# High and low activation rows in one product of 512 columns, in the hidden projections of a two-part transformer

## The chip, the core and the metric

The kernel runs on one core of a Trainium2 chip. The metric is the device time of one execution in microseconds. Lower is better.

## The reference, cut to what matters

Two blocks of a transformer follow each other on 256 tokens of width 1024. The change touches three kinds of projection from width 1024 to a hidden width: gate and up of the SwiGLU (width 2816, two layers), and the first projection of an MLP with squared relu (width 4096, two layers of the second block, one of them also on a second stream of 256 context tokens).

```python
def swiglu(h, w_gate, w_up, w_down):
    return (jax.nn.silu(h @ w_gate) * (h @ w_up)) @ w_down
...
        h = rms_norm(x, ffn_norm[i]) * (1.0 + sc_f) + sh_f
        x = x + g_f * swiglu(h, ffn_w_gate[i], ffn_w_up[i], ffn_w_down[i])
```

The MLP of the second block is relu(h @ w1) squared, times w2. Attention of three kinds, a pooling mixer and the modulation vectors (a vector c times large matrices) make up the rest. All is float32.

## The kernel before, in words

**Products.** A float32 product is made of three in the faster type fp32r: each operand is split into a high part (rounded) and a low part (the rest), and high x high, high x low and low x high are summed in PSUM (`three`, L1582 to L1586). Activations are turned so that the model width lies on the partitions: `hT_hi` and `hT_lo`, each 128 x 8 (k) x 256 tokens.

**Weights.** They stream in units of 1 MB, in the order of the segments `segs`. SP fetches unit u into one of four slots `wraw` as soon as the unit four before has been split. ACT rounds it to `whi` (L556, two halves of 1024), DVE subtracts for `wlo` (L945, two halves). `whi` and `wlo` have two slots, so a split of unit u + 2 waits until TensorE is done with unit u (`unit_done`), and TensorE waits for `lo_ready` of each half.

**Hidden units.** A unit of a gate, up or first projection is 1024 x 256 weights: 8 k-tiles by 2 halves f of 128 hidden columns. `hidden_unit` (L1631) makes for each f and k one triple with 128 x 128 weights as the stationary and 256 tokens as the moving operand; the results of both f lie side by side in one bank, in turn banks 2, 0, 1, 3 (`H_BANKS`). In the first unit of a stage k is the outer loop, since `hT` comes in by k (`fed_wait`); there a matmul of zeros (L1644) starts the bank. Stages `up0` and `up1` have kind "pair": gate and up units alternate, 22 in each stage; ACT reads the gate's bank with silu into `hbuf` (L573), DVE multiplies the up's bank by it (L962). Stages `up20`, `up21` and `up3` have kind "up", 16 units each: ACT reads the bank with relu into `hbuf` (L578) and squares it into `hid` (L581).

**Order on ACT and DVE.** Both are strict sequences. In `stream` (ACT and DVE), step i is: split unit i + 2, then the output of unit i, then, where the stage carries vector units, the next ring transfer (ACT) or a bias sum (DVE). In the last two steps of a stage the output comes first, then the split of the first two down units. A down unit also needs `act_hi` (ACT, L552) and `act_lo` (DVE, L939), the split of 512 hidden values, ahead of its weights.

**Vector units.** A piece of the modulation vectors (8 matmuls on 1 MB from the `ring`, which ACT fetches) stands behind each of the first 12 units of `up0`, 20 of `up1`, 12 of `up21` and 4 of `down1`.

**Down.** `down_segment` starts its four banks (4, 5, 6, 2) with matmuls of zeros (L1676) once the hidden stage's last ACT step is done, then per unit 24 products with `act_hi` or `act_lo` as the stationary and 512 weight columns as the moving operand. Ahead of a hidden stage stands a norm: `norm` on PE (L1698) turns the rows through banks 6, 0, 1, 3 (`T_BANKS`).

Of the kernel before, what the change touches and what calls it, by code (L numbers as in the profile page):

```python
# [8 lines left out]
F32R = mybir.dt.float32r  # L9
BF16 = mybir.dt.bfloat16  # L10
I32 = mybir.dt.int32
ALU = mybir.AluOpType
# [79 lines left out]
def build(nc, x, c, positions, ada_w, ada_b, attn_norm, ffn_norm, ffn_w_gate, ffn_w_up, ffn_w_down,  # L92
# [6 lines left out]
    with stack:  # L99
# [13 lines left out]
        hT_hi = sb("hT_hi", [P, KT, S], F32R)  # L113
        hT_lo = sb("hT_lo", [P, KT, S], F32R)
# [56 lines left out]
        T_BANKS = (6, 0, 1, 3)  # L171
# [113 lines left out]
        hid_done, hact_done = sem("hid_done"), sem("hact_done")  # L285
# [72 lines left out]
        HT_STEPS = (0, 1, 2, 4, 6)  # L358
        PLAIN = (4, 6)
# [150 lines left out]
        def _(act):  # L510
# [52 lines left out]
            def hidden_out(s_, i):  # L563
# [3 lines left out]
                if s_["kind"] == "pair":  # L567
# [3 lines left out]
                    act.wait_ge(unit_done, u + 1)  # L571
                    act.wait_ge(hid_done, hid_base[tag] + n - 1)
                    nc.scalar.activation(hbuf[:, n % 2, :], ps[:, H_BANKS[i % 4], :], ACT.Silu).then_inc(hact_done, 1)  # L573
                else:
                    act.wait_ge(unit_done, u + 1)
# [75 lines left out]
            def norm_columns():  # L651
# [3 lines left out]
                for b in (1, 3):  # L655
# [3 lines left out]
                    for k in (2 * b, 2 * b + 1):  # L659
                        shift = 0.0 if n in PLAIN else modT[:, l, strm, f, 0, k:k + 1]  # L660
                        ins = nc.scalar.activation(full[:, k, :], ps[:, T_BANKS[b], (k % 2) * S:(k % 2 + 1) * S], ACT.Identity,
# [224 lines left out]
        def _(dve):  # L886
# [65 lines left out]
            def hidden_out(s_, i):  # L952

                if s_["kind"] != "pair" or i % 2 == 0:
                    return
                u = s_["base"] + i
                n = i // 2
                hb = hid_base[s_["name"][2:]]
# [96 lines left out]
            def norm_columns():  # L1055
# [10 lines left out]
                def modulated(k):  # L1066
                    src = ps[:, T_BANKS[k // 2], (k % 2) * S:(k % 2 + 1) * S]
# [456 lines left out]
        def _(pe):  # L1524
# [106 lines left out]
            def hidden_unit(s_, i):  # L1631

                u = s_["base"] + i
                hb = hid_base[s_["name"][2:]]
                unit_wait(u, 0)

                if s_["kind"] == "pair":
                    which, v = (hact_done if i % 2 == 0 else hid_done), hb + i // 2 - 1
                else:
                    which, v = hact_done, hb + i - 3  # L1640
                pe.wait_ge(which, v)
                zeroed = i == 0
                if zeroed:
# [391 lines left out]
```

## Time and profile before

| | |
|---|---|
| three runs | 1711.67, 1711.74, 1712.48 us, median 1711.74 |
| profiled execution | 1709.29 us, span in the profile 1707.2 us |
| granted TensorE clock, mean | 0.941 |
| busy: PE, PEld | 1549.2 us (91%), 1308.6 us (77%) |
| busy: DVE, ACT | 938.3 us (55%), 718.6 us (42%) |
| HBM read | 333.79 MB, 196 GB/s over the span |

The profile is one execution. PE is TensorE's matmuls, PEld its weight loads, DVE is VectorE, ACT is ScalarE, SP the engine that issues the weight transfers. A matmul's duration reaches from its start to the end of its pipeline, so durations overlap; their distances do not. An idle time stands in brackets with what ended it.

### The profile page before, as it was taken

The page shows a single profiled execution, that of the slowest core. Times are in us where ns is not written, and L with a number is a line of the kernel's source. Part 1 is how long each engine was busy: PE and PEld are TensorE (multiplying, and loading weights), DVE is VectorE, ACT ScalarE, POOL GpSimd, SP SyncE. Part 2 cuts the span into 40 slices and gives each one's busy share as a digit, 9 for nine tenths or more (in the row PEclk, how much of TensorE's full clock was granted, in tenths as well). Part 3 has the DMA queues.
Part 4 walks back from the last instruction along what each step waited for, and adds up shares of the span by engine and source line. Part 5 has one row for each costly group of instructions (what it writes and reads, how often), then busy time and mean ns, then how long its engine had stood idle before and what let it go on. Part 6 is the DMA issues. An engine that isn't in the chain of part 4 may idle for free.

```text
span 1707.2 us, 24515 instructions
## 1 busy us (share of the span) xinstructions
PE 1549.2 (91%) x10326; PEld 1308.6 (77%) x10326; DVE 938.3 (55%) x1609; ACT 718.6 (42%) x1098; POOL 0.2 (0%) x4
## 2 busy tenths in 40 slices
PE   3998789999898789999979999799998886999997
PEld 2766668898686559888759988688986764779986
DVE  3584545345669755334575455753456786363455
ACT  2353524334444424333435544344444543345543
POOL 0000000000000000000000000000000000000000
PEclk9997789999998889999979999899999898989999
DMA  9962157965544657997734655469655353545552
GB/s 370 368 240 99 50 173 266 306 201 178 185 149 157 213 173 251 306 306 254 241 111 151 195 174 190 142 210 305 205 195 172 124 172 123 173 124 177 171 195 86
DMA packets 165845, 336.42 MB, mean 197 GB/s; under 512 B 8160, under 2 KB 109160, under 8 KB 165480
## 3 DMA queue, kind: packets, MB, share of 16 engines
q1 hardware_dynamic: 138880, 230.90, 40.2%
q10 hardware_dynamic: 26856, 103.96, 18.0%
q8 instruction: 81, 1.33, 0.3%
q14 instruction: 28, 0.23, 0.0%
HBM read 333.79 MB, written 1.05 MB: 196 GB/s over the span
## 4 chain that ended last, share of the span: by engine, by line
PE 79%; DVE 14%; ACT 2%; issue 2%; DMA 2%; ACTq 0%; SPq 0%; DVEq 0%
PE ps L1584 22%; PE ps L1585 21%; PE ps L1586 21%; PE ps L1556 5%; DVE wlo L945 2%; PE ps L1715 2%; DVE res L1024 1%; DVE work L1022 1%; PE ps L1712 1%; PE ps L1812 1%; PE ps L1785 1%; ACT whi L556 1%; PE ps L1824 1%; DVE work L1109 1%; PE ps L1754 1%
## 5 line engine op out<-in xcount | busy, mean ns | idle before, releaser
L945 DVE TENSOR_TENSOR wlo<-wraw,whi 128x1024 fp32r<-128x1024 f32 (+1 forms) x424 | 498.1, 1216 | 415.1 <-ACT whi L556 414.6
L556 ACT ACTIVATE whi<-wraw 128x1024 fp32r<-128x1024 f32 (+1 forms) x424 | 423.7, 1047 | 472.5 <-PE ps L1586 452.6
L1584 PE MATMUL ps<-hT_hi,whi 128*128 128x256 f32 x1472 | 422.5, 287 | 0.0
L1585 PE MATMUL ps<-hT_lo,whi 128*128 128x256 f32 x1472 | 416.9, 283 | 0.0
L1586 PE MATMUL ps<-hT_hi,wlo 128*128 128x256 f32 x1472 | 416.5, 283 | 0.0
L1584 PEld LDWEIGHTS ps<-hT_hi,whi 128*128 128x128 f32 x1472 | 282.8, 192 | 20.2 <-issue 18.1
L1585 PEld LDWEIGHTS ps<-hT_lo,whi 128*128 128x128 f32 x1472 | 282.9, 192 | 0.0
L1586 PEld LDWEIGHTS ps<-hT_hi,wlo 128*128 128x128 f32 x1472 | 282.8, 192 | 0.0
L1584 PE MATMUL ps<-whi,act_hi 128*128 128x512 f32 x560 | 219.0, 391 | 0.0
L1585 PE MATMUL ps<-wlo,act_hi 128*128 128x512 f32 x560 | 218.1, 390 | 0.0
L1586 PE MATMUL ps<-whi,act_lo 128*128 128x512 f32 x560 | 217.9, 389 | 0.0
L1584 PE MATMUL ps<-whi,hT_hi 128*128 128x512 f32 (+2 forms) x416 | 163.3, 393 | 5.2 <-DVE hT_lo L1073 5.1
L1585 PE MATMUL ps<-wlo,hT_hi 128*128 128x512 f32 (+2 forms) x416 | 159.1, 382 | 0.0
L1586 PE MATMUL ps<-whi,hT_lo 128*128 128x512 f32 (+2 forms) x416 | 158.4, 381 | 0.0
L939 DVE TENSOR_TENSOR act_lo<-work,act_hi 128x512 fp32r<-128x512 f32 x70 | 48.5, 693 | 191.7 <-ACT whi L556 191.7
L1584 PEld LDWEIGHTS ps<-whi,act_hi 128*128 128x128 f32 x560 | 105.1, 188 | 25.6 <-issue 3.8
L552 ACT ACTIVATE act_hi<-work 128x512 fp32r<-128x512 f32 x70 | 44.2, 631 | 191.2 <-issue 170.0
L1586 PEld LDWEIGHTS ps<-whi,act_lo 128*128 128x128 f32 x560 | 105.1, 188 | 22.0
L1585 PEld LDWEIGHTS ps<-wlo,act_hi 128*128 128x128 f32 x560 | 105.1, 188 | 21.5
L1584 PEld LDWEIGHTS ps<-whi,hT_hi 128*128 128x128 f32 x416 | 79.7, 191 | 30.9 <-issue 8.7
L1556 PE MATMUL ps<-ring,cpad 128*32 128x256 f32 x1440 | 97.9, 390 | 2.0 <-DMA ring<-in_ada_w_dram 1.2
L1586 PEld LDWEIGHTS ps<-whi,hT_lo 128*128 128x128 f32 x416 | 79.2, 190 | 15.3
(200 smaller groups left out, 1319.6 us busy)
## 6 DMA issues: line engine op xcount, KB each, us to landing
wraw<-in_mlp_w_dram SPq DMA_DIRECT2D x96, 1024.0 KB, 5.4
ring<-in_ada_w_dram ACTq DMA_DIRECT2D x90, 1024.0 KB, 5.6
wraw<-in_ffn_w_gate_dram SPq DMA_DIRECT2D x22, 1024.0 KB, 6.2
wraw<-in_ffn_w_up_dram SPq DMA_DIRECT2D x22, 1024.0 KB, 6.2
wraw<-in_ffn_w_down_dram SPq DMA_DIRECT2D x22, 1024.0 KB, 4.9
wraw<-in_diff_w_in_dram SPq DMA_DIRECT2D x12, 1024.0 KB, 5.0
wraw<-in_attn_w_qkv_dram SPq DMA_DIRECT2D x12, 1024.0 KB, 5.1
wraw<-in_sp_w_in_dram SPq DMA_DIRECT2D x8, 1024.0 KB, 13.0
```

The source lines that it names most:

```text
L552: nc.scalar.activation(act_hi[:, u % 2, :], hid[:, at:at + 512], ACT.Copy)
L556: nc.scalar.activation(whi[:, u % 2, part], raw_view(u)[:, part], ACT.Copy).then_inc(hi_ready, 1)
L939: nc.vector.tensor_tensor(act_lo[:, u % 2, :], hid[:, at:at + 512], act_hi[:, u % 2, :].bitcast(F32), ALU.subtract)
L945: nc.vector.tensor_tensor(wlo[:, u % 2, part], raw_view(u)[:, part], whi[:, u % 2, part].bitcast(F32), ALU.subtract).then_inc(lo_ready, 1)
L1022: nc.vector.tensor_tensor(tmp[:, t, cols], ps[:, D_BANKS[q], :], gate_b[:, cols], ALU.mult).then_inc(dve_emptied, 1)
L1024: nc.vector.tensor_tensor(res[:, strm, t, cols], res[:, strm, t, cols], tmp[:, t, cols], ALU.add).then_inc(sem("res_ready"), 1)
L1109: return nc.vector.tensor_tensor(views[t], views[t], g.rearrange("p a (c d) -> p a c d", c=1).to_broadcast([P, a, b, width]), ALU.mult)
L1556: ins = mm(ps[32 * c_:32 * c_ + 32, ADA_BANK, 0:256], cpad[:, 0 if g < 12 else 1, kt, :], ring_view(r)[:, kk * D + 256 * c_:kk * D + 256 * ...
L1584: mm(dst, s_hi, m_hi, start=start, stop=False, skip_group_check=skip)
L1585: mm(dst, s_hi, m_lo, start=False, stop=False, skip_group_check=skip)
L1586: return mm(dst, s_lo, m_hi, start=False, stop=stop, skip_group_check=skip)
L1715: ins = nc.tensor.transpose(ps[:, T_BANKS[b], (k % 2) * S + t * P:(k % 2) * S + (t + 1) * P], xn[:, t, k * P:(k + 1) * P], ident)
```

## The change

`hT_hi` and `hT_lo` become two halves of one tile `hT`, so that one moving operand can cover both: for a k, 256 high and 256 low columns. In a hidden unit high weights times high and low activations is now one product of 512 columns, which fills a whole bank; low weights times high activations stays one of 256 columns, added to the bank's first half. The two halves of the bank have to be added. DVE does this as it reads: a reduce over pairs of values 256 columns apart, for both f (two banks), into `hbuf` (gate and first projections) or `hid` (up). ACT's silu and relu read `hbuf` instead of PSUM and wait for the new semaphore `hid_sum`; the product of gate and up is made from SBUF. A unit takes two banks, in turn (0, 1), (2, 3), (4, 5). So the third unit waits for the copies of the gate vector out of banks 4 and 5, a unit from the fourth on for the sum of the unit three before, the down stage for the second-last sum only, and the transposes ahead of a hidden stage use banks 6, 3, 2, 4 (the last of them with a wait for the gate copies). The first unit needs no matmul of zeros.

```diff
-        hT_hi = sb("hT_hi", [P, KT, S], F32R)
-        hT_lo = sb("hT_lo", [P, KT, S], F32R)
+        hT = sb("hT", [P, 2, KT, S], F32R)
+        hT_hi, hT_lo = hT[:, 0], hT[:, 1]
...
+        HIDDEN_BANKS = (0, 2, 4)
+        TO_ROWS, TO_HIDDEN = (6, 0, 1, 3), (6, 3, 2, 4)
...
+        def hidden_banks(i):
+
+            b = HIDDEN_BANKS[i % 3]
+            return ps[:, b:b + 2, :].rearrange("p f (a n) -> p f n a", a=2)
...
-                    act.wait_ge(unit_done, u + 1)
                     b = i % 2
-                    act.wait_ge(hid_done, hid_base[tag] + i - 1)
-                    nc.scalar.activation(hbuf[:, b, :], ps[:, H_BANKS[i % 4], :], ACT.Relu).then_inc(hact_done, 1)
+                    act.wait_ge(hid_sum, sum_base[tag] + i + 1)
+                    nc.scalar.activation(hbuf[:, b, :], hbuf[:, b, :], ACT.Relu).then_inc(hact_done, 1)
...
-                if s_["kind"] != "pair" or i % 2 == 0:
+                if s_["kind"] == "down":
                     return
...
                 dve.wait_ge(unit_done, u + 1)
-                dve.wait_ge(hact_done, hb + n + 1)
-                at = 512 * n
-                nc.vector.tensor_tensor(hid[:, at:at + 512], ps[:, H_BANKS[i % 4], :], hbuf[:, n % 2, :], ALU.mult).then_inc(hid_done, 1)
+                if pair and i % 2:
+                    dst = hid[:, 512 * n:512 * n + 512]
+                else:
+                    dve.wait_ge(hid_done, hb + n - 1)
+                    dst = hbuf[:, n % 2, :]
+                nc.vector.tensor_reduce(dst.rearrange("p (f n) -> p f n", f=2), hidden_banks(i), AX, ALU.add).then_inc(hid_sum, 1)
+                if pair and i % 2:
+                    dve.wait_ge(hact_done, hb + n + 1)
+                    dve.wait_ge(hid_sum, sb_ + i + 1)
+                    nc.vector.tensor_tensor(dst, dst, hbuf[:, n % 2, :], ALU.mult).then_inc(hid_done, 1)
...
-                pe.wait_ge(which, v)
-                zeroed = i == 0
-                if zeroed:
-                    mm(ps[:, H_BANKS[0], :], zero16[0:1, 0:P], zero16[0:1, :], start=True, stop=False, skip_group_check=True)
...
+                if i >= 3:
+                    pe.wait_ge(hid_sum, sum_base[s_["name"][2:]] + i - 2)
+                if i == 2:
+                    pe.wait_ge(*gate_out[0])
...
-                    ins = three(ps[:, H_BANKS[i % 4], f * S:(f + 1) * S], whi[:, u % 2, c0:c0 + P], wlo[:, u % 2, c0:c0 + P], hT_hi[:, k, :], hT_lo[:, k, :],
-                                k == 0 and not zeroed, k == KT - 1 and not zeroed, zeroed)
+                    bank = HIDDEN_BANKS[i % 3] + f
+                    mm(ps[:, bank, :], whi[:, u % 2, c0:c0 + P], hT[:, :, k, :], start=(k == 0), stop=False, skip_group_check=True)
+                    ins = mm(ps[:, bank, 0:S], wlo[:, u % 2, c0:c0 + P], hT_hi[:, k, :], start=False, stop=(k == KT - 1), skip_group_check=True)
...
-                pe.wait_ge(hact_done, hb)
+                pe.wait_ge(hid_sum, sum_base[tag] + by_name["up" + tag]["count"] - 1)
```

The order of instructions on ACT at the end of `up3`, from the split of unit 15 to that of the second down unit (`down3`), before:

```order
L556 ACTIVATE whi<-wraw 128x1024 [waits unit_done,raw_full3]
L556 ACTIVATE whi<-wraw 128x1024
L578 ACTIVATE hbuf<-ps 128x512 [waits hid_done,unit_done]
L581 ACTIVATE work<-hbuf 128x512 [waits hact_done]
L578 ACTIVATE hbuf<-ps 128x512 [waits hid_done,unit_done]
L581 ACTIVATE work<-hbuf 128x512 [waits hact_done]
L552 ACTIVATE act_hi<-work 128x512 [waits hid_done,unit_done,raw_full0]
```

And in the changed kernel:

```order
L569 ACTIVATE whi<-wraw 128x1024 [waits unit_done,raw_full3]
L569 ACTIVATE whi<-wraw 128x1024
L589 ACTIVATE hbuf<-hbuf 128x512 [waits hid_sum]
L592 ACTIVATE work<-hbuf 128x512 [waits hact_done]
L589 ACTIVATE hbuf<-hbuf 128x512 [waits hid_sum]
L592 ACTIVATE work<-hbuf 128x512 [waits hact_done]
L565 ACTIVATE act_hi<-work 128x512 [waits hid_done,unit_done,raw_full0]
```

The order is the same; relu reads `hbuf` and waits for DVE's sum instead of TensorE's unit.

DVE at the same place, in the changed kernel (`work` in `act_lo<-work` is the hidden row `hid`). Before, the rows L978 were not there:

```order
L956 TENSOR_TENSOR wlo<-wraw,whi 128x1024 [waits hi_ready] x2
L978 TENSOR_REDUCE hbuf<-ps 128x512 [waits hid_done,unit_done] x2
L950 TENSOR_TENSOR act_lo<-work,act_hi 128x512 [waits hi_ready]
L956 TENSOR_TENSOR wlo<-wraw,whi 128x1024
L956 TENSOR_TENSOR wlo<-wraw,whi 128x1024 [waits hi_ready]
L978 TENSOR_REDUCE hbuf<-ps 128x512 [waits hid_done,unit_done]
L950 TENSOR_TENSOR act_lo<-work,act_hi 128x512 [waits hi_ready]
```

The two reduces of units 13 and 14 stand between the split of unit 15 and that of the first down unit, the reduce of unit 15 between the splits of the first and the second down unit.

## Rows read from the trace of the kernel before

**Rows 1.** The page's chain that ended last, by engine and by line.

```profile
PE 79%; DVE 14%; ACT 2%; issue 2%; DMA 2%; ACTq 0%; SPq 0%; DVEq 0%
PE ps L1584 22%; PE ps L1585 21%; PE ps L1586 21%; PE ps L1556 5%; DVE wlo L945 2%; PE ps L1715 2%; DVE res L1024 1%; DVE work L1022 1%; PE ps L1712 1%; PE ps L1812 1%; PE ps L1785 1%; ACT whi L556 1%; PE ps L1824 1%; DVE work L1109 1%; PE ps L1754 1%
```

**Rows 2.** Costliest groups: line, engine, op, forms, count | busy us, mean ns | idle before.

```profile
L945 DVE TENSOR_TENSOR wlo<-wraw,whi 128x1024 fp32r<-128x1024 f32 (+1 forms) x424 | 498.1, 1216 | 415.1 <-ACT whi L556 414.6
L1584 PE MATMUL ps<-hT_hi,whi 128*128 128x256 f32 x1472 | 422.5, 287 | 0.0
```

**Rows 3.** Timeline of PE in `up3`: start us, us, line, tiles.

```profile
1539.89 0.28 PE L1584 MATMUL ps<-hT_hi,whi 128*128 128x256 f32 x1
...
1551.05 0.28 PE L1584 MATMUL ps<-hT_hi,whi 128*128 128x256 f32 x1
```

**Rows 4.** Timeline of PE in `down3`.

```profile
1619.74 0.39 PE L1585 MATMUL ps<-wlo,act_hi 128*128 128x512 f32 x1
...
1623.82 0.39 PE L1585 MATMUL ps<-wlo,act_hi 128*128 128x512 f32 x1
```

**Rows 5.** Timeline of ACT in `up3`: [idle before <- releaser].

```profile
1539.07 2.01 ACT L556 ACTIVATE whi<-wraw 128x1024 fp32r<-128x1024 f32 x2 [2.60 <-PE ps L1586]
1540.99 0.57 ACT L578 ACTIVATE hbuf<-ps 128x512 f32<-128x512 f32 x1
...
1544.83 2.01 ACT L556 ACTIVATE whi<-wraw 128x1024 fp32r<-128x1024 f32 x2 [2.60 <-PE ps L1586]
```

**Rows 6.** Timeline of DVE in the same beat.

```profile
1540.17 2.36 DVE L945 TENSOR_TENSOR wlo<-wraw,whi 128x1024 fp32r<-128x1024 f32 x2 [3.40 <-ACT whi L556]
```

**Rows 7.** Timeline of ACT in `up21`, with vector units.

```profile
1123.17 2.01 ACT L556 ACTIVATE whi<-wraw 128x1024 fp32r<-128x1024 f32 x2 [3.21 <-PE ps L1586]
...
1125.69 0.38 ACTq L328 DMA_DIRECT2D ring<-in_ada_w_dram  x1
1130.11 2.01 ACT L556 ACTIVATE whi<-wraw 128x1024 fp32r<-128x1024 f32 x2 [3.79 <-PE ps L1586]
```

**Rows 8.** Groups of DVE by form: a reduce out of PSUM.

```profile
L1158 DVE TENSOR_REDUCE rowmax<-ps 128x2 f32<-128x1024 f32 x8 | 9.8, 1225 | 16.9 <-PE ps L1785 16.9
```

**Rows 9.** Timeline of DVE near the end of `up1`.

```profile
782.17 2.36 DVE L945 TENSOR_TENSOR wlo<-wraw,whi 128x1024 fp32r<-128x1024 f32 x2 [4.58 <-ACT whi L556]
784.44 0.68 DVE L962 TENSOR_TENSOR work<-ps,hbuf 128x512 f32<-128x512 f32 x1
```

**Rows 10.** Timelines from `up3` to `down3`: two rows of ACT, two of DVE, two of PE.

```profile
1602.37 0.60 ACT L578 ACTIVATE hbuf<-ps 128x512 f32<-128x512 f32 x1 [2.54 <-PE ps L1586]
...
1603.54 0.62 ACT L552 ACTIVATE act_hi<-work 128x512 fp32r<-128x512 f32 x1
...
1605.13 0.69 DVE L939 TENSOR_TENSOR act_lo<-work,act_hi 128x512 fp32r<-128x512 f32 x1 [5.01 <-ACT whi L556]
1605.74 2.35 DVE L945 TENSOR_TENSOR wlo<-wraw,whi 128x1024 fp32r<-128x1024 f32 x2
...
1609.82 0.50 PE L1584 MATMUL ps<-whi,act_hi 128*128 128x512 f32 x1
...
1615.43 0.39 PE L1584 MATMUL ps<-whi,act_hi 128*128 128x512 f32 x1
```

**Rows 11.** PE at the start of `up3`, and windows there: us, busy of the engines, PEclk.

```profile
1514.32 0.60 PE L1644 MATMUL ps<-zero 1*128 1x512 bf16 x1
1514.85 0.58 PE L1584 MATMUL ps<-hT_hi,whi 128*128 128x256 f32 x1
...
1516.86 0.28 PE L1584 MATMUL ps<-hT_hi,whi 128*128 128x256 f32 x1
...
1514.80:1516.90 2.10, 2.10 (x11) 2.05 (x11) 2.03 (x5) 2.07 (x4) 0.00 (x0) 0.54 0.00 0
```

**Rows 12.** DMA issues in 1120 to 1205 us: count, KB, median us to landing.

```profile
wraw<-in_mlp_w_dram SPq DMA_DIRECT2D x13, 1024.0 KB, 7.3
ring<-in_ada_w_dram ACTq DMA_DIRECT2D x12, 1024.0 KB, 5.5
```

More of the change, by code:

```diff
@@ L284, in build @@
                 n_ += s_["count"] // 2 if s_["kind"] == "pair" else s_["count"]
-        hid_done, hact_done = sem("hid_done"), sem("hact_done")
+        hid_done, hact_done, hid_sum = sem("hid_done"), sem("hact_done"), sem("hid_sum")
+        sum_base, n_ = {}, 0
+        for s_ in segs:
+            if s_["kind"] in ("pair", "up"):
+                sum_base[s_["name"][2:]] = n_
+                n_ += s_["count"]
+        def hidden_banks(i):
+            b = HIDDEN_BANKS[i % 3]
+            return ps[:, b:b + 2, :].rearrange("p f (a n) -> p f n a", a=2)
         VECTORS = 24
@@ L358, in build @@
         HT_STEPS = (0, 1, 2, 4, 6)
+        T_BANKS = [TO_HIDDEN if n in (1, 3, 5, 7, 10) else TO_ROWS for n in range(len(NORMS))]
         PLAIN = (4, 6)
@@ L660, in norm_columns @@
                         shift = 0.0 if n in PLAIN else modT[:, l, strm, f, 0, k:k + 1]
-                        ins = nc.scalar.activation(full[:, k, :], ps[:, T_BANKS[b], (k % 2) * S:(k % 2 + 1) * S], ACT.Identity,
+                        ins = nc.scalar.activation(full[:, k, :], ps[:, T_BANKS[n][b], (k % 2) * S:(k % 2 + 1) * S], ACT.Identity,
                                                    bias=shift, scale=modA[:, l, strm, f, k:k + 1])
@@ L1066, in modulated @@
                 def modulated(k):
[L1067 removed]
+                    src = ps[:, T_BANKS[n][k // 2], (k % 2) * S:(k % 2 + 1) * S]
                     if n in PLAIN:
@@ L1633, in hidden_unit @@
                 u = s_["base"] + i
-                hb = hid_base[s_["name"][2:]]
                 unit_wait(u, 0)
[L1637 to L1640, printed above, removed]
-                pe.wait_ge(which, v)
-                zeroed = i == 0
-                if zeroed:
-                    mm(ps[:, H_BANKS[0], :], zero16[0:1, 0:P], zero16[0:1, :], start=True, stop=False, skip_group_check=True)
-                for f, k in [(f, k) for k in range(KT) for f in range(2)] if zeroed else [(f, k) for f in range(2) for k in range(KT)]:
-                    if f == 0 and zeroed:
+                if i >= 3:
+                    pe.wait_ge(hid_sum, sum_base[s_["name"][2:]] + i - 2)
+                if i == 2:
+                    pe.wait_ge(*gate_out[0])
+                for f, k in [(f, k) for k in range(KT) for f in range(2)] if i == 0 else [(f, k) for f in range(2) for k in range(KT)]:
+                    if f == 0 and i == 0:
                         fed_wait(k)
@@ L1672, in down_segment @@
                 tag = s_["name"][4:]
-                hb = hid_base[tag] + by_name["up" + tag]["count"] // (2 if by_name["up" + tag]["kind"] == "pair" else 1)
-                pe.wait_ge(hact_done, hb)
+                pe.wait_ge(hid_sum, sum_base[tag] + by_name["up" + tag]["count"] - 1)
                 for q in range(4):
@@ L1708, in norm @@
                         pe.wait_ge(sem("xn_ready"), 4 * n + 2 + b)
+                    if b == 3 and T_BANKS[n] is TO_HIDDEN:
+                        pe.wait_ge(*gate_out[0])
                     for k in (2 * b, 2 * b + 1):
```

16 lines of the change are left out of this document (8 added, 8 removed).

## The prediction

> **What bounds the kernel now.** I read the chain of waits first. It runs 79% through TensorE, and 64% of the span is the three product lines L1584 to L1586 [rows 1]; the costliest groups say that 1472 triples of these have `hT` as the moving operand [rows 2]. These are the 92 hidden units (44 of gate/up, 48 of the first MLP projections; 2 halves x 8 k each). A matmul's mean duration (287 ns) is no price, since matmuls overlap; the price is the distance from start to start in the timeline. In a dense stretch of `up3` 93 products of 256 columns take 1551.05 - 1539.89 = 11.16 us, 0.120 us each [rows 3]; in the down projection 18 products of 512 columns take 4.08 us, 0.2267 us each [rows 4]. Twice the columns cost 1.89 times, so a part of each product (0.240 - 0.227 = 0.013 us) is paid per instruction.
>
> The unit's beat confirms it: ACT starts the split of one weight unit at 1539.07 and of the next at 1544.83 [rows 5], 5.76 us = 48 x 0.120. The reader should see that ACT waits 2.60 us there for TensorE, and that DVE's two splits take 2.36 us of the beat and it idles 3.40 us [rows 6]. With a vector unit of the modulation behind it the beat is 1130.11 - 1123.17 = 6.94 us [rows 7]; the vector unit is 1.18. So TensorE bounds every hidden unit, and the other two have room, on average. What matters is their order, below.
>
> **The change, part by part.**
>
> *Products.* A unit has 16 pairs instead of 16 triples: 16 x (0.2267 + 0.120) = 5.547 us instead of 5.76, 0.213 less. No row shows a product whose moving operand is two rows of 256 that lie apart. Lower bound of its cost: the plain 512 columns, 0.2267. Upper: two products of 256, 0.240, with no gain. I take 0.2267, since the columns are still read in runs of 256.
> The Trainium skill, page "TensorE: Matmul & The Clock Gate", section "Back-to-back issue gap", gives N/2.4 + 2.5 ns for one product, 109 and 216 ns here; by that the change would save 16 x 2.6 = 42 ns in a unit and not 213. This trace does not agree: 120 and 227 ns.
>
> *Zeroing.* The first unit of each of five stages loses a zero matmul, whose start lies 0.53 us ahead of the first product [rows 11]: 5 x 0.53 = 2.6 us. It stands right behind the transposes, so its time is on the path. The same rows show nine products in 2.01 us instead of 1.08, at a mean granted clock of 0.54, near the lower of the two levels (1.2 GHz); that cold start is there before and after.
>
> *Reduce.* DVE gets 92 reduces of 1024 values out of two banks. A PSUM reduce of 1024 to 2 takes 1.225 us [rows 8]. No row has one of 1024 to 512 with its two addends 256 columns apart. Lower bound 1.225 (as many values are read). Upper: 2.45, if every pair or every jump costs a second pass. I take 1.225, since DVE's subtraction that writes 1024 results costs no more (1.216 [rows 2]). ACT's silu and relu now read SBUF: as the 512-wide copy there, 0.62 and not 0.57 [rows 5, 10]: +0.05. The product of gate and up stays about 0.68 [rows 9].
>
> *The new order.* Before, ACT ran relu or silu as soon as it had split. Now it waits for a reduce that stands behind both of DVE's splits, and everything behind relu on ACT waits too: the square, the ring transfer, the next split. For the first projections this closes a loop from one split to the next:
> - ACT split to DVE split: 1540.17 - 1539.07 = 1.10 [rows 5, 6]
> - DVE two splits, to the start of what follows: 784.44 - 782.17 = 2.27 [rows 9]
> - reduce 1.225, and 0.05 until ACT starts
> - relu to the ACT instruction behind the square: 1603.54 - 1602.37 = 1.17, and 0.05 for SBUF [rows 10]
>
> Sum 5.87 us. That is more than the new TensorE beat (5.55) and than the old one (5.76). So in `up20` and `up3` the loop sets the pace, once TensorE has used up its lead, while the 12 units of `up21` with a vector unit (5.55 + 1.18 = 6.73) stay bound by TensorE. In gate/up only each second unit has ACT work behind the reduce: silu ends 1.10 + 2.27 + 1.225 + 0.05 + 0.62 = 5.3 us after the split began, under 5.55, and the odd unit's reduce and product hold nobody. All 44 stay with TensorE.
>
> *End of a stage without vector units*, counted from the end of unit 0. Before: unit 14 ends at 14 x 5.76 = 80.64, and the second down unit starts 1615.43 - 1602.30 = 13.13 later [rows 10] (unit 14 ended 0.07 ahead of its relu), at 93.8. After: the split of unit 15 starts at 13 x 5.87 = 76.3; DVE's reduce of 13 at +3.37 = 79.7, relu 80.95, relu of 14 at 82.2, `act_hi` 83.4, `act_lo` 1.59 behind it, 85.0, `wlo` 0.61 later, its first half ready 1.27 after that: the first down unit starts at 86.9 (before: 1609.82 - 1602.30 = 7.52 behind 80.64, 88.2). But DVE takes up unit 15's reduce only at 85.6 + 2.27 = 87.9; relu 89.1, `act_hi` 90.4, `act_lo` 92.0, `wlo` 92.6, ready at 93.8. TensorE is through with 24 products (5.44) at 92.3 and waits 1.5 us. The second down unit starts at 93.8, as before: **the whole gain in these stages is given back**, but for unit 0 (0.21) and the zeroing (0.53): 0.74 x 2 = 1.5 us.
>
> *The other stages.* `up21`: 15 units x 0.213 + 0.53 = 3.7, and by the same steps with little lag its second down unit comes 13.0 instead of 13.13 behind unit 14: 3.8 us. Gate/up: 44 x 0.213 = 9.4, zeroing 2 x 0.53: 10.4 us; there DVE's last reduce and product end before the first down unit does, nothing is late.
> *Edits at nothing.* Three pairs of banks and the banks of the transposes: a pair is reused three units later, its sum is ready within one. The waits on the gate copies: these are done before the transposes start. The down stage's wait for the second-last sum comes true during the last unit. The ring transfer moves from 2.5 us behind a unit's end [rows 7] to 5.4 (gate/up, even units: 4.7). It is needed 13.4 behind it; transfers land in 5.5 to 7.3 us [rows 12], so it is covered by 0.7 to 2.5 us.
>
> Sum: 10.4 + 3.8 + 1.5 = 15.7 us. The profiled execution took 1709.3 (span 1707.2), 2.4 under the median of the runs, 1711.7. Against it 1693.6; for the median I forecast **1696 us**.
>
> **Rivals.**
> *The reduce takes two passes* (2.45 us), place: DVE, behind the splits in `up20`, `up21` and `up3`. Loop 7.09 us; the split of unit 15 at 92.2, three slower reduces on the way, the second down unit at 113.3 instead of 93.8: +19.5 in each of two stages, less 0.74. `up21`: 113.3 against 107.9, +4.7. Gate/up: 11.9 us for two units without vector units (five times, against 11.52), -6 in all. Sum +36: **1748 us, slower**. For it: no such row. Against it: reads and writes of 1024 both cost 1.2. Each 0.1 us on the reduce costs 13 loops and 3 reduces in two stages, about 5 in the third, 37 times 0.1 = 3.7 us; it decides from 1.225 + 15.7/37 = 1.65 us on.
> *The product saves nothing* (0.240, its two rows cost like two products): the beat stays 5.76, only the zeroing is won, 2.6 us: 1709, no change. The skill's page named above leans this way, with 42 ns a unit. Against it: rows 3 and 4.
> *The ring transfer comes late.* If landing grew to 9 us with both streams starting together, TensorE would wait 1.0 us in each second unit of `up21` and 0.2 in 16 of gate/up: some 9 us, 1705, still faster.
> Besides, TensorE's new wait of 1.5 us ahead of the second down unit may lower its clock for a while: by rows 11 some 1 us each, three times.
>
> **How the numbers follow.** Forecast 0.77, two-pass reduce 0.10, no gain on the product 0.06, ring late 0.07. The range of the likeliest reaches down to a loop that costs nothing (92 x 0.213 + 2.6 = 22: 1690) and up to a reduce of 1.5 us (+10: 1706), and takes the late ring in; that holds 8 in 10. A measurement can tell about 0.2%, 3.4 us, from no change: faster 0.83, same 0.07, slower 0.10.
>
> **What would show it.** Start to start 0.227 and 0.120 in a hidden unit; the reduce at 1.22; splits on ACT 5.55 apart in gate/up and 6.73 with a vector unit, but 5.87 in `up20` and `up3`, with ACT's idle time now put down to DVE's reduce; 1.5 us of TensorE idle ahead of the second down unit. Wrong if the reduce is over 1.5 us, if the 512-column product starts over 0.24 apart, or if TensorE waits for the ring.

## The result and the profile after

The changed kernel takes **1700.5 us** (median of 4 runs, 1700.05 to 1701.97) against 1711.7 (4 runs, 1709.77 to 1712.48). The ratio of after to before is 0.9939, with a 95% interval of 0.9924 to 0.9954: 11 us faster, where 15.7 were forecast (1696, range 1690 to 1706).

The page of the changed kernel: span, engines, the head of the chain, and the group of the new reduce (out<-in, count | busy us, mean ns of one | idle before, releaser); the last line is a DMA issue (KB, median us to landing).

```profile
span 1698.5 us, 21648 instructions
PE 1533.6 (90%) x8849; PEld 1224.5 (72%) x8849; DVE 1044.4 (61%) x1701; ACT 724.0 (43%) x1098; POOL 0.2 (0%) x4
PE 66%; DVE 21%; ACT 6%; issue 3%; DMA 3%; ACTq 0%; SPq 0%; DVEq 0%
...
L978 DVE TENSOR_REDUCE hbuf<-ps 128x512 f32<-128x1024 f32 x70 | 85.1, 1218 | 2.1 <-PE ps L1668 2.1
...
ring<-in_ada_w_dram ACTq DMA_DIRECT2D x90, 1024.0 KB, 6.8
```

In [rows 1] TensorE had 79% of the chain; now it has 66%, and DVE, with its new reduce (1218 ns a piece, 22 of the 92 write `hid` and stand in a group of their own), has 21%. The span is 8.7 us shorter than that of the profiled execution before. To place these 8.7 us I measured each of the five stages that the change touches from its first hidden product to its last down product, in both traces, and the piece between the start of the transposes and the first product by itself:

| stage | before, us | after minus before |
|---|---|---|
| up0 + down | 202.72 | -0.73 |
| up1 + down | 216.76 | -1.59 |
| up20 + down | 181.23 | -0.35 |
| up21 + down | 195.51 | -0.84 |
| up3 + down | 181.96 | -0.37 |
| transposes to first product, five times | | -3.9 |
| all the rest, in this execution | | -0.9 |

The five stages together give 3.9 us, as much as the five zero matmuls alone. The forecast had 4.7 + 4.7 + 0.2 + 3.3 + 0.2 = 13.1 for the stages without the zeroing. So most of what is missing lies in the stages where TensorE sets the pace; the rest of this section shows how the parts read.

TensorE, `up20` and then `up3` of the changed kernel (start, duration of one, engine; each row is the first of a pair). In each stage 30 pairs lie between its first two rows. The third row of `up20` is the start of its last unit, seven units behind the first row; the last three of `up3` are the starts of units 13, 14 and 15:

```profile
939.82 0.40 PE L1667 MATMUL ps<-hT,whi 128*128 128x512 f32 x1
...
950.42 0.40 PE L1667 MATMUL ps<-hT,whi 128*128 128x512 f32 x1
...
979.40 0.40 PE L1667 MATMUL ps<-hT,whi 128*128 128x512 f32 x1
...
1539.78 0.39 PE L1667 MATMUL ps<-hT,whi 128*128 128x512 f32 x1
...
1550.18 0.39 PE L1667 MATMUL ps<-hT,whi 128*128 128x512 f32 x1
...
1580.00 0.46 PE L1667 MATMUL ps<-hT,whi 128*128 128x512 f32 x1
...
1585.77 0.50 PE L1667 MATMUL ps<-hT,whi 128*128 128x512 f32 x1
...
1591.58 0.50 PE L1667 MATMUL ps<-hT,whi 128*128 128x512 f32 x1
```

10.60 us for 30 pairs is 0.3533 a pair, 10.40 is 0.3467. The forecast had 0.3467 (0.2267 + 0.120); it is met in `up3`, while the other four stages run at 0.3533, 5.65 us for the 16 pairs of a unit (all but one unit of `up21`, see the last section). Inside a pair, in `up21` (one pair of three; spacings repeat every three pairs, and on average 0.2365 follows the wide product and 0.117 the narrow one):

```profile
1128.60 0.40 PE L1667 MATMUL ps<-hT,whi 128*128 128x512 f32 x1
1128.83 0.28 PE L1668 MATMUL ps<-hT,wlo 128*128 128x256 f32 x1
1128.94 0.40 PE L1667 MATMUL ps<-hT,whi 128*128 128x512 f32 x1
```

ACT, the first of a unit's two splits: a unit of gate/up behind another (beat 5.66), two units of `up21` with a vector unit each (6.84), and `up3` (5.81; brackets give the idle time before and what ended it):

```profile
368.57 2.01 ACT L569 ACTIVATE whi<-wraw 128x1024 fp32r<-128x1024 f32 x2 [0.39 <-PE ps L1668]
...
374.23 2.01 ACT L569 ACTIVATE whi<-wraw 128x1024 fp32r<-128x1024 f32 x2 [3.65 <-PE ps L1668]
...
1122.71 2.01 ACT L569 ACTIVATE whi<-wraw 128x1024 fp32r<-128x1024 f32 x2 [0.93 <-PE ps L1668]
...
1129.55 2.01 ACT L569 ACTIVATE whi<-wraw 128x1024 fp32r<-128x1024 f32 x2 [0.93 <-PE ps L1668]
...
1535.74 0.63 ACT L589 ACTIVATE hbuf<-hbuf 128x512 f32<-128x512 f32 x1 [2.61 <-DVE hbuf L978]
...
1536.94 1.99 ACT L569 ACTIVATE whi<-wraw 128x1024 fp32r<-128x1024 f32 x2
...
1541.55 0.63 ACT L589 ACTIVATE hbuf<-hbuf 128x512 f32<-128x512 f32 x1 [2.62 <-DVE hbuf L978]
...
1542.75 1.99 ACT L569 ACTIVATE whi<-wraw 128x1024 fp32r<-128x1024 f32 x2
```

Against [rows 5], where the split waited 2.60 us for TensorE, in `up3` it now starts without waiting, and relu waits 2.61 us for DVE's reduce. From split to split it is 5.81 us. On DVE the same loop reads:

```profile
1538.02 2.36 DVE L956 TENSOR_TENSOR wlo<-wraw,whi 128x1024 fp32r<-128x1024 f32 x2 [2.31 <-ACT whi L569]
1540.30 1.22 DVE L978 TENSOR_REDUCE hbuf<-ps 128x512 f32<-128x1024 f32 x1
```

The reduce follows the two splits without a gap: the products have long been there. 5.81 is above 5.55 and above the old 5.76, so ACT and DVE fall behind TensorE in these two stages, by 0.16 us a unit in `up20` and 0.26 in `up3`.

TensorE does not slow down at once. In `up20` it takes its units 5.65 us apart to the last one: (979.40 - 939.82) / 7. The first half of a unit's low weights is ready 3.07 us ahead of unit 2 there, and still 1.08 us ahead of unit 15. In `up3`, where TensorE is faster, that lead falls from 2.97 us to 0.10 at unit 13, and only the last units come at the loop's pace, 5.77 and 5.81 us apart. So the loop eats TensorE's lead inside the stage, and its price is paid at the end of it.

The end of `up3`, TensorE and then DVE, against [rows 10]:

```profile
1597.64 0.81 PE L1691 MATMUL ps<-zero 1*128 1x512 bf16 x3
...
1599.68 0.50 PE L1604 MATMUL ps<-whi,act_hi 128*128 128x512 f32 x1 [1.23 <-DVE wlo L956]
...
1606.62 0.50 PE L1604 MATMUL ps<-whi,act_hi 128*128 128x512 f32 x1 [1.20 <-DVE wlo L956]
```

```profile
1597.80 0.69 DVE L950 TENSOR_TENSOR act_lo<-work,act_hi 128x512 fp32r<-128x512 f32 x1 [2.88 <-ACT whi L569]
...
1600.68 1.22 DVE L978 TENSOR_REDUCE hbuf<-ps 128x512 f32<-128x1024 f32 x1
```

The reduce of unit 15 is taken up at 1600.68, behind the down unit's splits, and TensorE waits 1.20 us in front of the second down unit (forecast: 1.5). In `up20` TensorE is 1.84 us ahead of the kernel before when it starts the first down unit (counted from the stage's first product), and gives 1.49 of them back by the last. In `up3` it is 1.83 and 1.46, although its products were faster there.

The start of `up3`, transposes and first product. Before, in [rows 11], the first product came at 1514.85:

```profile
1503.21 3.67 PE L1732 MATMUL ps<-cst,work 128*128 128x128 f32 x16 [1.30 <-DVE work L1073]
1506.54 0.78 PE L1667 MATMUL ps<-hT,whi 128*128 128x512 f32 x1
```

3.33 us from the first transpose to the first product; before, the transposes started at 1510.72, so it was 4.13. The stage gains 0.80 here, and 0.82, 0.67, 0.81, 0.81 in the other four. Not all of it is kept. The first product now starts with more time at the lower clock ahead of it: over the first unit of `up3` the mean granted clock is 0.81 (before 0.86), over that of `up1` 0.92 (before 1.00). From its first product to unit 1 a stage takes 0.28, 0.38, 0.20, 0.07 and 0.22 us more than before, 1.15 us in all; `after_again` (below) has 1.48. The forecast had 0.213 less for each.

The rival of the late ring transfer shows twice in the edited stages of this execution, once in `up0` and once, for 0.45 us, in `up21`. (A wait of 1.0 us for the ring at 564 us, outside these stages, is there before too, with 1.2.)

```profile
296.67 1.07 PE L1576 MATMUL ps<-ring,cpad 128*32 128x256 f32 x16 [1.02 <-DMA ring<-in_ada_w_dram]
```

### The profile page after: what moved, and what is told of

Same layout as the page of the kernel before. It is cut to its first block, busy times and chain, and to the rows that moved or that the text cites. A ratio compares the mean times of both kernels' runs of the same rounds, so it can differ in the third digit from the quotient of the medians.

```text
span 1698.5 us, 21648 instructions
## 1 busy us (share of the span) xinstructions
PE 1533.6 (90%) x8849; PEld 1224.5 (72%) x8849; DVE 1044.4 (61%) x1701; ACT 724.0 (43%) x1098; POOL 0.2 (0%) x4
## 3 DMA queue, kind: packets, MB, share of 16 engines
q10 hardware_dynamic: 26856, 103.96, 16.9%
q8 instruction: 70, 1.15, 0.3%
## 4 chain that ended last, share of the span: by engine, by line
PE 66%; DVE 21%; ACT 6%; issue 3%; DMA 3%; ACTq 0%; SPq 0%; DVEq 0%
PE ps L1667 13%; PE ps L1604 11%; PE ps L1605 11%; PE ps L1606 11%; DVE wlo L956 7%; PE ps L1668 6%; PE ps L1576 4%; ACT whi L569 3%; DVE hbuf L978 2%; PE ps L1732 2%; DVE res L1044 1%; DMA ring<-in_ada_w_dram 1%; DVE work L1042 1%; ACT hbuf L589 1%; PE ps L1729 1%
## 5 line engine op out<-in xcount | busy, mean ns | idle before, releaser
L1667 PE MATMUL ps<-hT,whi 128*128 128x512 f32 x1472 | 529.2, 403 | 0.0
L1668 PE MATMUL ps<-hT,wlo 128*128 128x256 f32 x1472 | 413.5, 281 | 0.0
L1667 PEld LDWEIGHTS ps<-hT,whi 128*128 128x128 f32 x1472 | 278.3, 189 | 85.3 <-issue 18.1
L1668 PEld LDWEIGHTS ps<-hT,wlo 128*128 128x128 f32 x1472 | 279.4, 190 | 0.0
L1604 PE MATMUL ps<-whi,hT 128*128 128x512 f32 (+2 forms) x416 | 163.1, 392 | 6.4 <-DVE hT L1093 6.4
L1605 PE MATMUL ps<-wlo,hT 128*128 128x512 f32 (+2 forms) x416 | 159.2, 383 | 0.0
L1606 PE MATMUL ps<-whi,hT 128*128 128x512 f32 (+2 forms) x416 | 158.5, 381 | 0.0
L1604 PEld LDWEIGHTS ps<-whi,act_hi 128*128 128x128 f32 x560 | 105.1, 188 | 30.8 <-DVE wlo L956 6.3
L1604 PEld LDWEIGHTS ps<-whi,hT 128*128 128x128 f32 x416 | 79.8, 192 | 32.0 <-issue 9.1
L1606 PEld LDWEIGHTS ps<-whi,hT 128*128 128x128 f32 x416 | 79.4, 191 | 15.3
L1605 PEld LDWEIGHTS ps<-wlo,hT 128*128 128x128 f32 x416 | 79.6, 191 | 14.0
L978 DVE TENSOR_REDUCE hbuf<-ps 128x512 f32<-128x1024 f32 x70 | 85.1, 1218 | 2.1 <-PE ps L1668 2.1
```

The source lines that it names most:

```text
L978: nc.vector.tensor_reduce(dst.rearrange("p (f n) -> p f n", f=2), hidden_banks(i), AX, ALU.add).then_inc(hid_sum, 1)
L1604: mm(dst, s_hi, m_hi, start=start, stop=False, skip_group_check=skip)
L1605: mm(dst, s_hi, m_lo, start=False, stop=False, skip_group_check=skip)
L1606: return mm(dst, s_lo, m_hi, start=False, stop=stop, skip_group_check=skip)
L1667: mm(ps[:, bank, :], whi[:, u % 2, c0:c0 + P], hT[:, :, k, :], start=(k == 0), stop=False, skip_group_check=True)
L1668: ins = mm(ps[:, bank, 0:S], wlo[:, u % 2, c0:c0 + P], hT_hi[:, k, :], start=False, stop=(k == KT - 1), skip_group_check=True)
```

## The experiments

All are variants of the changed kernel. They ran beside the kernel before on the same chip: the first four against 1711.8 us (17 runs), the next four against 1711.52 (11 runs), the two repeats at the end on another chip against 1711.16 (one run). My theory was: the product's extra 0.0067 us a pair comes from its moving operand or its order, the stages that gain nothing owe this to the ACT-DVE loop, and the gain is given back at their ends.

**Are the two far rows of 256 columns the cost?** In `a_contig` the high and low row of one k lie side by side, so that the product reads 512 columns in one run.

```diff
-        hT = sb("hT", [P, 2, KT, S], F32R)
-        hT_hi, hT_lo = hT[:, 0], hT[:, 1]
+        hT = sb("hT", [P, KT, 2, S], F32R)
+        hT_hi, hT_lo = hT[:, :, 0], hT[:, :, 1]
...
-                    mm(ps[:, bank, :], ..., hT[:, :, k, :], ...)
+                    mm(ps[:, bank, :], ..., hT[:, k, :, :], ...)
```

> The changed kernel with hT laid out as 8 k x 2 x 256, so that the 512 moving columns of a high product are contiguous. The changed kernel's profile shows a pair of products (512 and 256 columns) every 0.3533 us in four of five stages and every 0.3467 in the last. Theory 1, the two far rows of the moving operand cost 0.007 us a product: the pair takes 0.347 everywhere, the beat in gate/up falls from 5.65 to 5.55 us, 56 TensorE-bound units give 6 us, 1694.5 us. Theory 2, the start of a product falls on one of two grids for the whole stage, whatever it reads: 0.3533 or 0.3467 by stage as before, though perhaps in other stages, and the time stays within 1698 to 1702.

Measured: 1700.15 us (ratio 0.9924, 0.9907 to 0.9942), the same as the changed kernel. TensorE in `up3`, 30 pairs:

```profile
1544.94 0.40 PE L1667 MATMUL ps<-hT,whi 128*128 128x512 f32 x1
...
1555.54 0.40 PE L1667 MATMUL ps<-hT,whi 128*128 128x512 f32 x1
```

0.3533 a pair, in all five stages. Far rows cost nothing. And `up3`, which had run at 0.3467, was now at 0.3533, although only a layout had changed.

**Is it the alternation of 512 and 256 columns?** In `b_order` two k go together: two products of 512, then their two of 256 (`wide` is `(bank, c0, k)`).

```diff
+                    if i == 0:
+                        late = [wide]
+                    elif k % 2 == 0:
+                        late = [wide]
+                        continue
+                    else:
+                        late.append(wide)
-                    ins = mm(ps[:, bank, 0:S], wlo[:, u % 2, c0:c0 + P], hT_hi[:, k, :], ...)
+                    for bank_, c_, k_ in late:
+                        ins = mm(ps[:, bank_, 0:S], wlo[:, u % 2, c_:c_ + P], hT_hi[:, k_, :], ...)
```

> The changed kernel with another order of products: in a half, the two high products of k and k + 1 follow each other, then their two low-weight products of 256 columns (512, 512, 256, 256). Theory 1 (far rows cost): four products take 0.707 us as now, 1700.5. Theory 2 (grid of starts after an alternation of 512 and 256): the spacings change; 0.693 us for four products if the grid is left, and 1694 to 1696 us; if the change of length costs at each switch, fewer switches give the same sign.

Measured: 1696.83 us (0.9907, 0.9883 to 0.993; 1689.98 to 1703.22). TensorE's beat fell to 5.57 us, and to 6.79 with a vector unit; ACT's splits stayed 5.81 apart in `up20` and `up3`. The five stages give 8.0 us instead of 3.9 (5.1 in `after_again`, which had no wait for the ring in them). So the order of widths moves the pace, and the loop does not care about it. That alternation as such costs time is not shown: `up3` of the changed kernel alternates too and had 5.55.

**What does the reduce cost alone?** `c_three` takes the wide product back: two products of 256 into the two halves of the bank. Reduce, order and pairs of banks stay.

```diff
-                    mm(ps[:, bank, :], whi[..], hT[:, :, k, :], ...)
+                    mm(ps[:, bank, 0:S], whi[..], hT_hi[:, k, :], ...)
+                    mm(ps[:, bank, S:2 * S], whi[..], hT_lo[:, k, :], ...)
```

> The changed kernel with the product change alone undone: high weights by high and by low activations are again two products of 256 columns, into the two halves of the bank; the reduce, its waits, the three pairs of banks and the missing zeroing stay. If the ACT-DVE loop of 5.81 us sets the pace of the two first-projection stages without vector units, they take no longer than in the changed kernel; only the 44 gate/up units and the 12 with vector units get their beat of 5.76 us back, 56 x 0.107 = 6 us more: 1706.5. If the loop did not matter, all 92 units would: 10 us more, 1710. If the product saved its full 0.213 us somewhere unseen: 1712.

Measured: 1711.2 us (12 runs, 1705.16 to 1715.35; 0.9994, 0.9981 to 1.0008), no gain; I had expected 1706.5. ACT in `up20`:

```profile
935.91 1.99 ACT L569 ACTIVATE whi<-wraw 128x1024 fp32r<-128x1024 f32 x2
...
940.51 0.63 ACT L589 ACTIVATE hbuf<-hbuf 128x512 f32<-128x512 f32 x1 [2.61 <-DVE hbuf L978]
...
941.72 1.99 ACT L569 ACTIVATE whi<-wraw 128x1024 fp32r<-128x1024 f32 x2
```

5.81 us from split to split, exactly as in the changed kernel, with a TensorE that needs 5.76 instead of 5.65 or less. Two kernels with different products and the same beat on ACT: in `up20` and `up3` ACT's pace is the loop's and not TensorE's. The five stages cost 1.55 us more than before. Between this kernel and an execution of the changed one with 0.3533 in every stage (`after_again`, below) lie -1.9, -2.0, -0.7, -1.3 and -0.7 us. Their sum, 6.65 us, is what the wide product is worth in the stages, where the forecast had a gain of 13.1 over the kernel before. The medians lie further apart, and missed my 1706.5; the mean granted clock, treated below, goes with that.

**Does the loop open if DVE reduces first?** `d_first` moves the reduce of a unit ahead of the splits two units later.

```diff
                 for i in range(s_["count"]):
+                    hidden_out(s_, i)
                     if i < s_["count"] - 2:
                         split_unit(s_["base"] + i + 2)
-                    hidden_out(s_, i)
```

> The changed kernel with one order changed on DVE: the reduce of unit i stands ahead of the split of unit i + 2, not behind it. The sum is then ready 1.3 us after a unit's end, when ACT is through with its own split, and the loop is open: ACT 3.1 us and DVE 3.5 us per beat. Theory (loop): beats of 5.81 fall to TensorE's 5.65 in up20 and up3, 13 x 0.16 = 2.1 us each at least, less 0.4 for the end of the stage, so 3.4 in all and 1697; the ring's transfers are issued 2 to 3 us earlier and its two waits (1.0 and 0.45 us) go: 1695.5. Rival (TensorE bound everywhere, the loop only fills idle time): 1700.5.

Measured: 1697.51 us (0.9909, 0.9892 to 0.9927); I had expected 1695.5 to 1697. ACT and DVE in `up20`:

```profile
934.69 2.01 ACT L569 ACTIVATE whi<-wraw 128x1024 fp32r<-128x1024 f32 x2 [2.45 <-PE ps L1668]
936.61 0.61 ACT L589 ACTIVATE hbuf<-hbuf 128x512 f32<-128x512 f32 x1
...
940.35 2.01 ACT L569 ACTIVATE whi<-wraw 128x1024 fp32r<-128x1024 f32 x2 [2.47 <-PE ps L1668]
```

```profile
934.63 1.23 DVE L978 TENSOR_REDUCE hbuf<-ps 128x512 f32<-128x1024 f32 x1 [2.13 <-PE ps L1668]
935.78 2.36 DVE L956 TENSOR_TENSOR wlo<-wraw,whi 128x1024 fp32r<-128x1024 f32 x2
```

The split waits for TensorE again and relu waits for nothing; the beat is 5.65 in `up20` (5.55 in `up3`). In the edited stages no ring transfer is waited for. TensorE still waits 0.62 and 0.75 us before the second down units of `up20` and `up3`, so the end of the stage still gives something back. Against `after_again`, `up20` is 1.0 us shorter although TensorE takes its units at the same 5.65: the gain is all at the end.

**Long runs.** `b8_runs` carries `b_order` to its end: for a half, 8 products of 512, then 8 of 256.

```diff
-                for f, k in ...:
-                    mm(..whi.., hT[:, :, k, :], ...)
-                    ins = mm(..wlo.., hT_hi[:, k, :], ...)
+                for f in range(2):
+                    for k in range(KT): mm(..whi.., hT[:, :, k, :], ...)
+                    for k in range(KT): ins = mm(..wlo.., hT_hi[:, k, :], ...)
```

> The changed kernel with the products of a half in two runs: first the eight high products of 512 columns (k = 0 to 7), then the eight low-weight products of 256, instead of alternating. If each switch of length costs (0.2365 instead of 0.2267 from a 512 to a 256), only two of 32 spacings are switches: 16 pairs take 5.55 us, the gate/up beat falls from 5.65 to 5.55, and the time by 56 x 0.1 = 5.6 us, 1695. If it is a grid that holds for a stage whatever the order, some stages stay at 5.65 and the gain is under 3 us. TensorE now needs the second half of the weights 0.5 us earlier in a unit, which costs nothing where it is ready ahead and up to 0.5 us a unit where the loop of 5.81 us holds.

Measured: 1698.39 us (0.9923, 0.9909 to 0.9937), above the expected 1695. TensorE in `up20` (one row is 8 products, the second number their common duration):

```profile
930.70 2.00 PE L1667 MATMUL ps<-hT,whi 128*128 128x512 f32 x8
932.54 1.12 PE L1677 MATMUL ps<-hT,wlo 128*128 128x256 f32 x8
933.49 2.00 PE L1667 MATMUL ps<-hT,whi 128*128 128x512 f32 x8
```

2.79 us for 8 pairs, 0.349 a pair, and a beat of 5.59 on TensorE: no better than `b_order`, and as there ACT's splits are 5.81 apart in the two stages of the loop. So few switches of width do not bring 5.55 either. Its stage sum is -8.0 too; the two medians differ by less than their intervals.

**The end of the stage.** `f_ends` is `d_first`, but behind the last unit of an `up` stage ACT and DVE first split for the second down unit and then do relu and reduce.

```diff
+                    early = s_["kind"] == "up" and i == s_["count"] - 1
+                    if early:
+                        split_unit(s_["base"] + i + 2)
                     hidden_out(s_, i)
...
-                    if i == s_["count"] - 2 or ...:
+                    if not early and (i == s_["count"] - 2 or ...):
```

> The kernel with the reduce ahead of the split on DVE, and in the last step of a first-projection stage the other way round on both engines: the split of the second down unit ahead of the output of the last hidden unit. The down stages of that kernel still start their second unit late (0.89, 0.52 and 0.98 us between the start and the end of the three down stages, against before). Theory: these 2.4 us go, and nothing else moves, since the last hidden row is read only at the end of the down stage: 1695 us. Rival: the late second unit is TensorE's clock after the short idle time, not DVE's order; then it stays at 1697.5.

Measured: 1694.37 us (0.9893, 0.9873 to 0.9914), as expected (1695). The second down unit's lateness, which `d_first` still had (0.89, 0.52 and 0.98 us in the three `up` stages), is 0.00, 0.02 and -0.02. What was given back at the end is thus recovered by order alone. The five stages give 13.7 us here, but part of that is luck: this execution had pairs at 0.3467 us in two stages, and `f_again` below did not.

**A dearer reduce.** `e_twice` adds a second reduce of the same 1024 values in the three `up` stages, into two spare columns.

```diff
+                if s_["kind"] == "up":
+                    nc.vector.tensor_reduce(spare[:, i % 2, :], ps[:, HIDDEN_BANKS[i % 3]:HIDDEN_BANKS[i % 3] + 2, :], AX, ALU.add)
                 nc.vector.tensor_reduce(dst.rearrange(...), hidden_banks(i), AX, ALU.add)
```

> The changed kernel with a second reduce over the same two banks, into a spare of two columns, ahead of each real one in the three first-projection stages. It computes nothing more that is used. The prediction's price for the reduce: 13 loops and 3 reduces in each of two stages and about 5 in the third, 37 times the added time. One more reduce stands 1.17 us on DVE: the loop goes from 5.81 to 6.98 us, and the time by 43 us to 1744. If the loop is not what sets the pace there (DVE is busy only 61% of the time), the time stays near 1700.

Measured: 1740.46 us (1.0164, 1.0151 to 1.0178), expected 1744. ACT in `up20`, beat 6.93:

```profile
935.63 1.99 ACT L570 ACTIVATE whi<-wraw 128x1024 fp32r<-128x1024 f32 x2
...
941.36 0.63 ACT L590 ACTIVATE hbuf<-hbuf 128x512 f32<-128x512 f32 x1 [3.75 <-DVE hbuf L981]
...
942.56 1.99 ACT L570 ACTIVATE whi<-wraw 128x1024 fp32r<-128x1024 f32 x2
```

Relu waits 3.75 us instead of 2.61 for DVE. Here the loop does set TensorE's pace: its units are 6.94 us apart from unit 5 of `up20` on. `up20` is 17.6 us longer than before, `up3` 16.9, `up21` 3.6; the rival of the two-pass reduce had 19.5, 19.5 (less 0.74) and 4.7 for these. Its mechanism is real, only its condition was not: one reduce costs 1.218.

**Both edits.** `g_both` is `f_ends` with the runs of `b8_runs`.

> Both of the others together: reduce first, ends in the other order, and the products of a half in two runs. If the switches of length cost, the beat is 5.55 in all stages and all 92 units are bound by TensorE: 92 x 0.1 = 9 us under the kernel with the orders alone, 1686. If the grid holds, 1692 to 1695.

Measured: 1693.32 us (1688.34 to 1696.62; 0.9889, 0.9874 to 0.9905), with a beat of 5.59 in every stage (6.78 with a vector unit). It has the lowest median, 18 us under the kernel before; from `f_ends` it can't be told apart. Its five stages give 14.9 us. The forecast of 1686 would have needed a beat of 5.55.

**The same kernel again.** `after_again` is the changed kernel, `f_again` is `f_ends`, each run once more and profiled, to see whether the pace of a stage belongs to the program.

> The changed kernel once more, for a second profile. If the two beats of the alternating products (5.65 and 5.55 us a unit) belong to the build, the stages show what they showed: 5.65 in gate/up, 0.3533 us a pair in up20 and 0.3467 in up3. If they are drawn anew in each execution, at least one stage changes, and the loop-bound stages stay at 5.81 either way.

> The kernel with the reduce first and the ends in the other order once more, for a second profile. It had 5.55 us in both stages without vector units, while the same kernel without the other end order had 5.65 in up20. If the beat belongs to the build: 5.55 and 5.55 again. If it is drawn in each execution: perhaps 5.65 in one of them, 0.1 us on each of 15 units.

Measured: 1701.93 and 1699.74 us. TensorE in `up3` of `after_again`, 30 pairs:

```profile
1544.78 0.40 PE L1667 MATMUL ps<-hT,whi 128*128 128x512 f32 x1
...
1555.38 0.40 PE L1667 MATMUL ps<-hT,whi 128*128 128x512 f32 x1
```

of `f_ends`:

```profile
1539.80 0.40 PE L1671 MATMUL ps<-hT,whi 128*128 128x512 f32 x1
...
1550.20 0.40 PE L1671 MATMUL ps<-hT,whi 128*128 128x512 f32 x1
```

and of `f_again`:

```profile
1544.79 0.40 PE L1671 MATMUL ps<-hT,whi 128*128 128x512 f32 x1
...
1555.38 0.40 PE L1671 MATMUL ps<-hT,whi 128*128 128x512 f32 x1
```

The same program shows 0.3533 in one execution and 0.3467 in another, so the pace is not fixed by the program. These two executions were on different chips, but the chip alone does not decide either: on one chip `a_contig` had 0.3533 in all stages, `f_ends` 0.3467 in two, and `d_first` both in one execution. The five stages of `f_again` give 9.7 us and not 13.7, so some 4 us of `f_ends` do not belong to its edit. `after_again` gives 5.1. Between these two, on one chip and both at 0.3533 in `up20` and `up3`, the two edits of the order are worth 4.6 us.

## Why the prediction was right, and where not

The sign and the range were right; the forecast was 4.5 us too low. By its own steps:

- **Products: the term that was mis-sized.** Forecast 5.547 us a unit and a gain of 0.213. Measured 16 x 0.3533 = 5.65, a gain of 0.107 against the old 5.76; with a vector unit 6.94 went to 6.85, 0.09. In `up0`, `up1` and `up21` 56 units behind the first are bound by TensorE, 41 of them with a vector unit: 5.3 us instead of 11.9, so 6.6 us of the 15.7 are missing here. The two durations were each right in a dense stretch of their own shape; set alternately they take 0.3533 (or 0.3467) together, and in blocks of eight 0.349. The upper bound of 0.240 for the wide product was not reached: it takes 0.2365 there, and the narrow one behind it 0.117. The Trainium skill's formula (page "TensorE: Matmul & The Clock Gate", section "Back-to-back issue gap"), which the section gives for an isolated product, led to an estimated gain of 0.042 a unit; the measured 0.107 lies between it and my 0.213, and the trace agrees with neither.
- **The first unit of a stage.** Forecast to gain 0.213 like the others. It lost 0.07 to 0.53 us. Its products start earlier, and more of them fall under the lower granted clock; where the clock was higher, in `up3` of `f_ends` (0.94), that unit took 0.56 us less than before. In the three stages bound by TensorE the loss is 1.4 us against the forecast (1.7 in `after_again`); over all five, about a third of what the piece with the zeroing gives is lost again.
- **Zeroing.** Forecast 0.53 each, measured 0.67 to 0.82, 3.9 us in all instead of 2.6. The zero matmul also stood some 0.3 us behind the transposes, which the distance of the two starts in [rows 11] did not show.
- **Reduce.** 1.225 forecast, 1.218 measured. Taken from the nearest row of the same operation and the same 1024 values read; no cost of the distance between the addends shows.
- **The loop.** 5.87 forecast, 5.81 measured on ACT, in exactly the two stages named. `c_three` (same beat, slower TensorE), `d_first` (beat back to TensorE's) and `e_twice` (beat 6.93) show that it is this loop. "In `up20` and `up3` the loop sets the pace, once TensorE has used up its lead" came true only in part: TensorE never used up its lead in `up20`, and in `up3` only at unit 13. What the loop took, it took at the end of the stage.
- **The end of a stage.** "The whole gain is given back": forecast -0.21 without the zeroing, measured -0.35 and -0.37. TensorE's wait before the second down unit was 1.20 us, forecast 1.5. `f_ends` takes it away by order alone. In `up21` the forecast had 0.1 us gained at this place; about 0.1 was lost, as its down stage took 0.5 us longer. The feared drop of the clock after this wait did not come: the granted clock stayed at 1.00 (2.4 GHz) behind it. In `e_twice`, behind idle times of 2.4 to 3.5 us at the starts of the down stages, it was 0.66 over the next 5 us.
- **Ring.** Forecast as covered by 0.7 to 2.5 us, with a rival at 0.07. Part of the rival came true: the landing grew from 5.6 to 6.8 us (the page's medians), and TensorE waited 1.02 and 0.45 us. That cost 1.5 us, not the rival's 9, and it belongs to this execution: `after_again` has the longer landing (6.6) too, but no such wait in the five stages. In `d_first`, where relu and with it the transfer's issue come earlier again, the landing is back at 5.7.
- **The two-pass reduce.** Did not happen. `e_twice` puts its price at 40 us over the changed kernel for 1.22 us of added reduce in three stages, 3.3 us for each 0.1 us, where the prediction had 3.7.

Corrected for this execution, the sum is 15.7 - 6.6 (products) - 1.4 (first units) - 1.5 (ring) + 1.3 (zeroing) + 0.3 (`up20` and `up3`, which gained more than forecast) - 0.2 (end of `up21`) = 7.6 us; for `after_again`, without the ring and with 1.7 for the first units, it is 8.8. The stages of the two executions give 3.9 and 5.1 us and the transposes' piece 3.9, together 7.8 and 9.0.

The medians lie 11.2 apart, and the other 2 to 3 us go along with the mean granted clock of the runs. Within one kernel the time falls by about 1.1 us for each 0.001 of the mean granted clock (my least-squares fit to the 85 recorded runs whose clock is on record). The changed kernel and `a_contig` have a mean of 0.943 in 11 runs, the kernel before 0.940 in 29, 11.7 us apart in mean time. Brought to one clock, an estimate of 8 us is left, which the edited pieces account for. `c_three`, at 0.940, lies 7 us above the changed kernel by the same working, where its stages say 6.65. So the edited work is worth about half of the 15.7, and the median's nearness to the forecast owes about 3 us to a clock that the forecast does not name; without them it would be near 1704, still inside the range. Whether the change or chance raised the mean clock stays open.

## What to carry to other kernels

When partial sums move from TensorE to another engine's reading, follow the instruction that now waits for the sum and all that is queued behind it on its engine; here one loop of ACT and DVE took most of the gain of two stages, without slowing TensorE before their ends, and moving the reduce ahead of the splits, and the next split ahead of the last reduce, brought 4.6 us in the stages, two thirds of what the wide product itself is worth. Take the price of a product from its own shape in its own neighbourhood: two spacings, each read in a uniform stretch, need not add up when the shapes alternate. A saving of a tenth of a microsecond per unit has to be followed to the stage's last unit before it is counted. And work that starts sooner under the lower clock also runs slower: time won ahead of a stage has to be followed into its first unit.

## What the hardware showed that I had not expected

**Two paces for alternating products.** Pairs of 512 and 256 columns start 0.3533 or 0.3467 us apart, one or the other mostly for a whole stage, and not the same in two executions of one program; in the first execution of the changed kernel one unit of `up21`, at 1145 to 1150 us, also had 0.3467. It was the unit behind TensorE's wait for the ring at 1143.59; the next one had 0.3533 again. Products of 256 alone kept 0.120 and blocks of eight 0.349. It is neither the layout (`a_contig`) nor the ACT-DVE loop (`d_first` has 5.65 in one stage and 5.55 in another). It is not the chip alone either, since both paces occur on one chip and in one execution. What sets it stays open; that it changed right behind a wait is one case and no proof.

**Stretches that nobody edited move by more than the edits.** The same work between two stages, with the granted clock in the third column from the end: before, changed kernel, and the changed kernel again.

```profile
1080.20:1112.70 32.50, 22.82 (x98) 16.60 (x97) 24.85 (x65) 11.60 (x26) 0.00 (x0) 0.76 0.32 110
```

```profile
1075.30:1106.10 30.80, 20.11 (x97) 15.11 (x97) 24.69 (x65) 11.60 (x26) 0.00 (x0) 0.84 0.33 116
```

```profile
1076.70:1109.30 32.60, 23.32 (x98) 16.88 (x96) 25.02 (x65) 11.60 (x26) 0.00 (x0) 0.77 0.32 110
```

The first number behind the stretch is its length: 32.5 us at a mean granted clock of 0.76, 30.8 at 0.84, and 32.6 at 0.77 for the very program that had 30.8. TensorE's level changes at another moment of the same work, between 1.2 and 2.4 GHz, and with it the stretch is 1.7 us longer or shorter. That goes either way, so a difference of 3 us between two single profiles of this kernel says nothing about an edit; the sums over the edited stages, read from first to last product, are what the verdicts above rest on.
